# A gated delta recurrence inside a two-block model: the table that sets every engine's order within a block of 16 beats is laid anew

## What is computed

```
def chunk_gated_delta(q, k, v, g, beta, s0):          # chunks of 64 tokens, 4 heads of 128
    gcum = jnp.cumsum(g, axis=-1)
    decay = jnp.exp(jnp.where(incl, gcum[..., :, None] - gcum[..., None, :], -jnp.inf))
    kb = k * beta[..., None]
    lower = jnp.where(strict, jnp.einsum('bhnid,bhnjd->bhnij', kb, k) * decay, 0.0)
    tinv = triangular_solve(eye + lower, eye)         # inverse of a 64x64 lower triangle
    u = tinv @ (v * beta[..., None])
    w = tinv @ (kb * jnp.exp(gcum)[..., None])
    attn = jnp.where(incl, jnp.einsum('bhnid,bhnjd->bhnij', q, k) * decay, 0.0)
    def step(S, inp):                                 # one chunk after the other
        v_new = ui - wi @ S
        o = qd @ S + ai @ v_new
        S = S * gl[..., None, None] + jnp.einsum('bhcd,bhce->bhde', kd, v_new)
        return S, o
```

## Time and profile before

| | |
|---|---|
| three runs | 3117.58 us median, 3112.32 to 3121.73 |
| the profiled execution | 3118.14 us, span of its instructions 3116.0 us |
| TensorE (PE) busy over the span | 2921.5 us, 94% |
| VectorE / ScalarE / GpSimd busy | 1539.8 / 588.8 / 864.5 us |
| mean granted TensorE clock | 0.979 of full speed |
| first instruction of the phase to its last | 2278.73 to 2527.50 us, about 249 us |

### The profile page before, as it was taken

The page is one execution under the profiler, slowest core; times in us unless marked ns, Lnnn a source line. Parts: engine busy times, 40 slices in busy tenths (PEclk is TensorE's granted clock), DMA queues, the critical chain, the costliest instruction groups (busy, mean ns, idle before and its releaser), DMA issues. The chain is left out here.

```text
span 3116.0 us, 52923 instructions
## 1 busy us (share of the span) xinstructions
PE 2921.5 (94%) x22406; PEld 2027.5 (65%) x22406; DVE 1539.8 (49%) x2520; ACT 588.8 (19%) x1102; POOL 864.5 (28%) x591
## 2 busy tenths in 40 slices
PE   9999999998999799999999998999878897999998
PEld 6855866896888477667666685677767644443433
DVE  5765746435465477434877664764644322111112
ACT  2133041003000344211000002221543211110101
POOL 1212112111121455211999790111355300000000
PEclk9999999999999899999999999999999988999999
DMA  4242323220331000132344452132200026999996
GB/s 167 82 162 82 90 80 110 85 77 28 97 119 55 9 4 4 66 112 82 128 129 149 145 168 79 58 102 74 70 9 3 22 106 263 382 409 409 409 409 265
DMA packets 122232, 412.67 MB, mean 132 GB/s; under 512 B 13568, under 2 KB 21376, under 8 KB 121744
## 3 DMA queue, kind: packets, MB, share of 16 engines
q1 hardware_dynamic: 112784, 373.64, 34.1%
q0 software_dynamic: 9216, 35.66, 3.6%
HBM read 404.97 MB, written 4.28 MB: 131 GB/s over the span
## 5 line engine op out<-in xcount | busy, mean ns | idle before, releaser
L947 PE MATMUL ps<-arena 128*128 128x256 f32 x4760 | 1045.3, 381 | 18.0 <-PEq L905 6.8
L947 PEld LDWEIGHTS ps<-arena 128*128 128x128 f32 x4760 | 899.9, 191 | 173.9 <-issue 43.7
L1003 PE MATMUL ps<-arena 128*128 128x512 f32 (+1 forms) x752 | 290.5, 544 | 10.4 <-DVE arena L1342 7.3
L885 POOL TENSOR_TENSOR arena<-arena 128x512 f32<-128x512 f32 x68 | 95.0, 1396 | 552.9 <-DMA arena<-in_w_in 195.3
L1003 PEld LDWEIGHTS ps<-arena 128*128 128x128 f32 x752 | 143.0, 192 | 149.9 <-issue 139.7
L3982 PE MATMUL ps<-arena 128*64 128x512 f32 x1024 | 224.8, 594 | 10.8 <-DMA arena<-in_w_up 8.4
L891 POOL TENSOR_TENSOR arena<-arena 128x512 f32<-128x512 f32 x68 | 87.3, 1284 | 484.5 <-PE ps L947 484.5
L1247 DVE TENSOR_TENSOR arena<-ps,arena 128x256 f32<-128x256 f32 x85 | 36.1, 424 | 335.1 <-PE ps L947 334.0
L1178 DVE SCALAR_TENSOR_TENSOR arena<-ps,params,arena 128x511 f32<-128x511 f32 (+4 forms) x266 | 190.7, 717 | 13.5 <-ACT arena L1079 4.4
L4126 POOL TENSOR_SCALAR arena<-arena,small 128x1024 f32<-128x1024 f32 x64 | 191.5, 2992 | 11.3 <-DMA arena<-in_w_mod 7.6
L1096 ACT ACTIVATE arena<-ps 128x256 f32<-128x256 f32 x85 | 32.3, 380 | 801.4 <-PE ps L947 487.1
(11 more groups left out here) (465 smaller groups left out, 4005.7 us busy)
## 6 DMA issues: line engine op xcount, KB each, us to landing
arena<-in_w_in SPq DMA_DIRECT2D x166, 512.0 KB, 3.8
arena<-in_w_gate SPq DMA_DIRECT2D x128, 512.0 KB, 15.5
arena<-in_w_up SPq DMA_DIRECT2D x128, 512.0 KB, 15.2
arena<-in_w_down SPq DMA_DIRECT2D x128, 512.0 KB, 15.6
arena<-in_w_mod POOLq DMA_DIRECT2D x48, 512.0 KB, 4.3
arena<-in_ffn_up SPq DMA_DIRECT2D x44, 512.0 KB, 4.0
arena<-in_w_branch SPq DMA_DIRECT2D x32, 512.0 KB, 3.7
arena<-spill POOLq DMA_DIRECT2D x16, 640.0 KB, 5.4
```

The costliest lines, as they stand in the source:

```text
L885: vec.tensor_tensor(plane(u, n), part(u, 1, 0), part(u, 1, 1), ALU.add).then_inc(sem, 1)
L947: last = nc.tensor.matmul(k.bank(b)[:, 0:HT], lhs[:, q * P:(q + 1) * P], rhs[:, q, :], start=(first and q == 0), stop=(q == 3), skip_group ...
L1003: last = nc.tensor.matmul(out[0:j["m"], 0:j["n"]], w[:, q * m:(q + 1) * m], j["rhs"](q), start=(n == 0), stop=(n == kn - 1))
```

## The change

Three tables of numbers and five places that go with them get new beats. No operation is added or removed, and no size changes.

```
-    PREPARE = {0: ["R"], 4: ["KK"], 9: ["QK"], 10: ["XT0"], 12: ["X0"]}
-    SOLVE = {0: ["Y5"], 1: ["kt0"], 2: ["XT5"], 3: ["kt1"], 4: ["vt0"], 5: ["vt1"], 7: ["U0"], 8: ["U1"], 10: ["W"], 12: ["E0"], 14: ["E1"]}
+    PREPARE = {1: ["R"], 4: ["KK"], 11: ["XT0"], 13: ["QK"], 14: ["X0"]}
+    SOLVE = {0: ["Y5", "kt0"], 1: ["XT5"], 3: ["kt1", "vt0", "vt1"], 5: ["U0"], 7: ["U1"], 9: ["W"], 11: ["E0"], 15: ["E1"]}
...
-    A_BEAT = [1, 2, 3, 5, 6, 7, 9, 10, 11, 13, 14, 15]
+    A_BEAT = [0, 1, 1, 4, 6, 6, 7, 10, 10, 13, 14, 15]
...  ScalarE: the two factors
-                    if b < GROUPS and beat == 1:
+                    if b < GROUPS and beat == 2:
...  GpSimd: the mask MB
-                        if beat == 0:
+                        if beat == 1:
...  GpSimd: X = LS times a mask
-                        if beat == 6:
+                        if beat == 7:
...  GpSimd: the diagonals for E0 and E1
-                        if lat(g) and beat in (9, 13):
-                            ti = int(beat == 13)
+                        if lat(g) and beat in (10, 12):
+                            ti = int(beat == 12)
```

## The result

The changed kernel takes 3082.46 us (median of 4 runs, 3081.71 to 3089.91) against 3117.47 us, a ratio of 0.9896 with a 95% interval of 0.9876 to 0.9915: faster by 35.0 us, where 24.6 were forecast and 31 were the most that the range allowed. The profiled execution took 3082.54 us, its span is 3080.5.

What follows compares the result with a forecast made beforehand. The phase was taken as bound by TensorE plus its waits; 23.7 us of waits and 1.7 us of clock make 25.4, so 3118.1 - 25.4 = 3092.7, given as 3093 us, range 3086 to 3106.

Steps and rivals of the forecast that it cites:

- The waits: TensorE's waits in the phase, 35.5 us with 6.7 fixed in block 1: 23.7 us were to go.
- XT behind ACT: XT waiting for ACT's copy of Y, 10.4 us in 11 waits, blocks 1, 2, 3 and 5: gain 8.6 us.
- chunk_u: chunk_u waiting for DVE, 11.2 us in 8 waits: gain 9.4 us, with 0.9 left heading blocks 4 and 6.
- the old X0 wait: X0 waiting for DVE's E0, 1.7 us in 2 waits: all gained; a new wait in blocks 2, 3, 5 loses 1.0.
- No operation comes or goes, so the work of TensorE stays: TensorE's busy time in the phase was taken as unchanged; only its waits would change.
- The clock: Block 5, behind the 2.35 us wait: half clock for 3.42 us, of which 1.7 us was counted as regained.
- Blocks 0 and 7 to 9 stay: These blocks were to keep their times: block 7 hardly waits, blocks 8 and 9 have only unmoved beats.
- DVE and POOL: Meeting in block 4, `scaled` takes 3.06 against 1.29 us; by the skill's lock rule up to POOL's run, 3.28 us.
- POOL's queue: Rival: waits for POOL in the phase replace those removed, about 12 us saved, 3106 us; chance 0.12.
- hidden otherwise: Rival: TensorE's work in the five blocks is partly hidden by an unseen chain, 3112 to 3118 us; chance 0.08.
- The clock falls more often: Rival: each further half-clock stretch in the phase costs 1.7 us, two give 3096; no separate chance given.
- slower: Rival: the chain with MB behind LM2 on POOL makes XT0 late in five blocks, 3130 us; chance 0.04.

Runs made afterwards that it cites:

- after: The changed kernel itself, with the whole change, against the kernel before: ratio 0.9896, median 3082.46 us.
- split: Changed kernel with the transpositions kt1, vt0 and vt1 apart again (beats 3, 4 and 5): ratio 0.9908 to the kernel before.
- before: The kernel without the change, the base of all ratios: 3117.47 us.
- before_shift: Kernel before with four more memsets on DVE at the start of the phase, moving all behind them: ratio 1.0016.
- levels_only: Kernel before with the beats of the levels (A_BEAT) alone changed: ratio 0.9968.
- rest_only: Changed kernel with the old beats of the levels; prepare, solve, masks and diagonals stay moved: ratio 0.9975 to the kernel before.
- x1_early: Kernel before with X1 moved from beat 3 to beat 2, ahead of `scaled` on DVE: ratio 0.9965.
- e_apart: Kernel before with E0 at beat 11, E1 at beat 15 and POOL's diagonals at 10 and 12: ratio 0.9982.
- idle: Changed kernel with six more POOL operations ahead of the second diagonal of block 5, making E1 wait: ratio 0.9917 to the kernel before.
- x1_late: Changed kernel with X1 back at beat 3, behind `scaled` on DVE: ratio 0.9903 to the kernel before.
- fill_moved: Changed kernel with block 8's fills at beats 1, 2, 5, 6, ... instead of 0, 2, 4, 6, ...: ratio 0.9874 to the kernel before.
- both_moved: Changed kernel with block 8's fills moved and chunk_u 0 behind Y5 and kt0 in blocks 4, 6 and 8: ratio 0.9875 to the kernel before.

## Why the prediction was right and where it was wrong

**What bounds the phase** was right: TensorE plus its waits. Block 4 is now all busy, and blocks 4 to 6 came to 30.2, 23.6 and 35.5 us where 31, 23.7 and 36 were said.

**The waits** were right in sum (24.1 us against 23.7) and by class: XT behind ACT 10.4 to 2.2 (8.2 gone, 8.6 said), chunk_u 11.2 to 1.8 (as said), E 5.1 to 0 (as said), the old X0 wait gone and a new one of 0.3 where up to 1.0 was said. What is left of them is mostly where the text put it: XT's two waits in block 1 (0.7 each), 0.25 behind Y4 in blocks 2 and 3 and at XT1 in block 6, chunk_u's at the heads of blocks 4 and 6. That the sum came so close is in part luck. The prediction says that 0.3 stays behind Y4 in blocks 2, 3 and 5 but does not take it off (10.4 - 3.0 + 1.2 is 8.6 only without it, 7.7 with it); the 0.8 of XT0 in block 1, counted among what stays, made up for it. "More than a dozen short waits" in blocks 2 to 4 are eleven and the one of 3.25 us.

**"No operation comes or goes, so the work of TensorE stays"** failed: a term put at nothing, which measured some 3 us. The two traces of each kernel, with half of the half-clock time taken off the phase, give 238.5 and 238.6 us before, 211.0 and 211.5 after: 27.3 us, 3.2 more than the 24.1 of waits. 1.3 us is the row of three transpositions, shown by the starts in after and split. Of the other 1.9 us the likely part is that a wait costs more than is printed: XT can start 0.65 after the copy's start and stands 1.41 after Y's start, 0.79 behind the end of Y's 0.62, and 0.72 is printed, because the record of a step runs on into the wait. Some 16 waits fewer make about 1.1 us of it. That was argued from rows and not tried by itself; the last 0.8 us is open.

**"The clock"** is the step that failed by most: one fall of 3.42 us, 1.7 us to win. The single trace showed one fall in blocks 2 to 7, but it was one of several places where it could come. In the seven traces of before and of kernels that keep most of its waits (before twice, before_shift, levels_only, rest_only, x1_early, e_apart), and in idle, which put one back, the clock fell in blocks 2 to 7 every time, for 3.4 to 17.1 us: at or closely behind the 2.35 us wait of block 5 (in all five traces that have it), at those of 3.25 and 2.60 us in blocks 4 and 6 (in two of four), once behind 1.05 and 0.61 us close together, and in idle at the wait put back. In the six that keep few (after twice, x1_late, split, fill_moved, both_moved) it never did, though x1_late still has waits of 1.90 us. Over all runs the mean clock is 0.9799 before and 0.9820 after, 5.2 us by the line above (give or take 2), against the 1.7 counted. The difference at equal clock, 28.3 us, and these 5.2 make 33.5, which with the scatter of the runs covers the 35.0 measured. How much of the 5.2 us belongs to the waits is open. Not all of it stands in the phase: behind it there are 37.2 and 32.1 us of half clock in the two traces before and 28.5 and 31.8 in the two after, in a stretch that the change does not touch; but fill_moved and both_moved, which also keep few waits, have 37.2 and 36.6 there, so four traces are too few to give that part to the change. Of the 10.4 us beyond the forecast of 24.6, then, 3.5 are the clock's, 3.2 the steps' and 0.4 the waits'; the other 3.3 lie within the scatter of the runs.

**"Blocks 0 and 7 to 9 stay"** held for the order and not for the pair of traces: 4.7 us of the first pair's difference were the clock in blocks 8 and 9, where a fall at chunk_state's waits comes and goes with the execution. That part of the 35.0 is luck of the pair.

**DVE and POOL.** The bound that the prediction gave for `scaled`, held up for as long as POOL's run of operations lasts, is not what the traces show. In x1_late the pair (2350.02 to 2352.47) begins and ends inside a run of three on POOL:

```profile
2349.18 4.18 POOL L3555 TENSOR_TENSOR arena<-arena 128x512 f32<-128x512 f32 x3 [1.44 <-ACT arena L3524]
```

In block 4 of the changed kernel the pair took 2.14 us, so that VN's subtraction behind it was held up for less than the walk had.

**The rivals**: POOL's queue did not take the place of the waits (Y1 and chunk_u wait for nothing of POOL's), and no part was hidden otherwise. "The clock falls more often" was weighed only as a loss; that it could fall less often than in the one trace, in the phase and outside, was not among them, and this side is where the time came out. The price of "slower" was also off: at 12.5 us of delay a block its own terms (8.9 us over the margin, five blocks, on 3092.7) give 3137 and not 3127 to 3130. The range, too, stopped at all waits and one fall, with 1.5 us for the scatter of runs that in truth differ by up to 20.

## What to carry to other kernels

Cut the stretch at its steps, sum the waits of the bounding engine, and ask of each what stands behind its releaser in the queue and what could stand in front of it: that sum came true within half a microsecond, if partly by luck. Then add what a wait costs beyond its own length: where the bounding engine is TensorE, each longer wait (2.35 us and more here), and here and there a shorter one (0.95 us in block 8, a cluster in rest_only), may come with 3 to 10 us at half clock in some executions. So one trace may show too few falls, and the mean clock of many runs is to be compared as well, though it did not follow the waits in every kernel here. A schedule is changed as a whole: half of this one gave a third of the gain, the other half a seventh, since steps moved without their neighbours uncover other waits.

## What the runs showed of the hardware that was not expected

- The same wait of 3.25 us left the granted clock at full (2.4 GHz) in one execution and fell together with 6.8 us at half (1.2 GHz) in another whose phase starts after four more memsets, while two waits of 1.05 and 0.61 us close together stood ahead of a fall in rest_only, and six falls stood at single waits of 0.95 us in block 8. The Trainium skill, "TensorE: Matmul & The Clock Gate", "HAM oscillation — how this bites in real kernels", ties the fall to idle time, and "A second HAM failure mode: psum-queue depth-cycling" to frequent short idles. The traces agree with the first by the waits of 2.35 us and more; for the second there are rest_only and block 8, more than the prediction gave it, but no run counts how many short idles it takes.
- A step of four transpositions of 128x128 cost 0.49 us in a row (1.46 for three steps) and 0.59 us alone between other shapes, in block 3.
- DVE's pair of full-width operations took 1.29 us with POOL idle, and 2.14, 2.45 and 3.06 us with POOL at work beside it, in four places of three kernels. What sets which of the three it is, no run separates.
